# A two-layer hybrid trunk on one core: the key norm moved on VectorE, the chunk inverse packed to 32 columns

## The chip, the cores and the metric

One core of a Trainium2 chip runs the whole program. The metric is the device time of one execution in microseconds; with one core there is no slowest core to choose. Before the change it is 1543.94 us, the median of three runs (1543.90 to 1547.18).

## The reference, cut to what matters

The input x has 512 tokens of 1024 float32 numbers. Two layers run one after the other, each with a projection into two head groups, an output projection and a squared-ReLU MLP of width 4096, with residual adds. Layer 0 has an RWKV-7 group (8 heads of 64) and a gated DeltaNet group (8 heads of 64); layer 1 has sparse attention and block attention. The change touches layer 0 alone.

Both groups of layer 0 are recurrences over the tokens. The kernel computes them in chunks of 64 tokens. Of DeltaNet's form the reference says it plainly: with a lower triangular matrix of 64 x 64 per head and chunk,

```
a_mat = where(strict, (k_beta @ k.T) * decay, 0) + eye(64)
u = solve(a_mat, v * beta);  w = solve(a_mat, k_beta * exp(g))
v_new = u - w @ S;  o = (q * exp(g)) @ S + qk @ v_new
S = S * exp(g_last) + (k * exp(g_last - g)).T @ v_new
```

RWKV-7 in chunks has a matrix of the same shape (RWKV's own products instead of k_beta and k). Its key kk is divided by its length per head (`l2_normalize(k * k_k)`), and b = kk * a. The "bonus" adds sum(r * k * r_k) * v per head to its output.

## The kernel before, in words

Every engine has its own program, written out by hand, and semaphores tie them together; the order inside an engine's queue is fixed. Activations lie feature by feature: 128 features on the partitions, 512 tokens along them.

**The even projection.** 31 tiles of 128 columns go through PE (`tile`, L503, L504, L508: each weight is split by ACT into a high part, L1045, and by POOL into a low part, L1984; 24 matmuls of 512 columns). SP loads the weight of tile u once POOL has split tile u - 2 (L421). PE's order (L544 to L610) is: two LoRA tiles, ab, K, the LoRA products (L575), the gate products (L579), R, V, the chunk sums (L585 to L589, 32 moving columns), GQ (4 tiles), head sums for kk (`head_sums0`, L540), GK (4 tiles), head sums for gq, GV tile 0 (tile 23), the bonus sums (L540), the other GV tiles, head sums for gk, Z. There are 8 PSUM banks in turn; fill q waits until fill q - 8 has been read, so the last of the four bonus sums waits for ACT's first read of the gq sums (L1051), and the first three for DVE's convolutions of GK 1 to 3. DVE convolves each tile (`convolved`, L1453, L1469, L1471). ACT's queue is in the order of its loop over x (from L1076): at x = 20 to 23 the rounding of tile x + 3 (waits for PE's tile x), then the silu of GK tile x - 20 (L1064); at x = 23 also the squares of GK (L1059) and the inverse norm of gq (L1051 logarithm, L1054 exponential). At x = 19 it does the inverse norm of kk. DVE's three operations with that norm (kk scaled, L1545; b, L1546; a product of 128 x 32, L1548) stand behind the convolution of GK tile 0; the squares of kk, and then its norm, lie in the place of GV. Then come GK 1 to 3, GV 0, the bonus products (L1552) and the scaling of GQ (L1554).

**POOL's constants.** Between tile_lo(3) and tile_lo(6) POOL builds masks (L1967 to L2022): for each of six levels of the inverse a mask of 128 x 128 (a memset and selects), then MERGE, the six of them cut to each half's own 64 columns (L2018), and three small ones. Each waits for the one before.

**The even mixer** goes over blocks of 128 tokens (s = 0 to 3, with an extra turn for the tail). In each turn all engines interleave the matrices and inverse of block s ("ahead") with the state steps and outputs of block s - 1 ("behind"). A tile "by head" is 128 x 512: partition halves are the two chunks of the block, 8 heads of 64 columns. LTR and LTG hold the matrices of RWKV (R) and DeltaNet (G).

**The inverse** joins diagonal blocks: from blocks of 2 rows on to 64 in five levels (LEVELS = 6, the first is free). At the start DVE masks LTG and LTR to the first off-diagonals (L1630, L1641), POOL adds the identity (L2052), and DVE transposes Q into TI (L1652, `first_inverse`). Each level then does, for R and then G:

```
PE   below_blocks : bank[g] = LT.T-products with TI     (both_halves, L640, 16 matmuls 64x64 by 64x64)
ACT  below_blocks : XM = -bank[g]                       (L1189)
PE   joined_blocks: bank[g] = Q-products with XM        (L640)
DVE  joined_blocks: TI = where(mask, bank[g], TI)       (L1659), later Q = transpose(TI) (L1664)
```

The last level writes into Q itself, and `inv_done` then lets `turned_inputs` of the next block and `solved` go on. On DVE the joins of levels 1 to 4 stand between the outputs of block s - 1: `chunk_out` (L1698 to L1704), `decay_steps` (L1606), `out_var`, `out_scaled` (L1717, L1718), `scaled_rows` (L1611, L1612), `mixed` (from L1724). PE's state sums and chunk outputs of block s - 1 stand between levels 0 and 1. ACT's copy of the key values (L1175) stands ahead of `solved(m, 1)` and of the levels.

## Time and profile before

| | us |
|---|---|
| median of three runs | 1543.94 |
| the profiled execution | 1542.63 |
| its span | 1540.7 |
| busy: PE / DVE / ACT / POOL | 1440.3 / 677.3 / 605.4 / 571.3 |
| even projection, to PE's first matmul of the mixer | 0 to 220 |
| a projected tile: PE / DVE's convolution of it | 5.5 / 3.75 |
| mixer, starts of blocks s = 0, 1, 2, 3 | 220.0, 255.2, 305.1, 356.5 |
| mixer's end, output projection's first matmul | 443.3 |
| mean granted clock of TensorE over the span | 0.97 |

The profiled execution's time holds 1.9 us around its span. Engines overlap, so busy times don't add up to the span. A row of a timeline can merge several records ("x64"); a PE record's duration runs from its start to its modelled end, so the records of a batch overlap, and the step from one to the next is their total less the last one's duration, over one less than their number. Each matmul of 32-bit numbers leaves two records.

### The profile page before, as it was taken

To read this page: it belongs to the slowest core of one execution; us is meant where nothing else is said; L and a number is where in the kernel's file an instruction comes from. 1 tells how busy PE (TensorE), PEld (TensorE's weight loads), DVE (VectorE), ACT (ScalarE), POOL (GpSimd) and SP (SyncE) were. 2 spreads that over 40 slices of the span, in tenths; PEclk is the share of its full clock that TensorE was granted. 3 is DMA by queue.
4 is the path that set the end of the run, shared out by engine and by line. 5 is a ranking of instruction groups with operands and counts; after the bars stand their busy time and mean duration, and the time that the engine had idled before them with its cause. 6 is when DMAs were issued, how large, how long until landed. Compare 5 with 4: busy or idle time off the path is not lost.

```text
span 1540.7 us, 24474 instructions
## 1 busy us (share of the span) xinstructions
PE 1440.3 (93%) x10273; PEld 1153.7 (75%) x10273; DVE 677.3 (44%) x1059; ACT 605.4 (39%) x872; POOL 571.3 (37%) x265
## 2 busy tenths in 40 slices
PE   7999899888769999999999799978999999999998
PEld 5787568788758888888888687754468888888886
DVE  4675756777543413223143306868823314122231
ACT  5425453434354413223142435467834313232231
POOL 4543321101024343434334232417934343434341
PEclk9999899999779999999999899998999999999999
DMA  4332200000112323232323221210012323223231
GB/s 141 96 96 68 69 14 3 3 3 3 57 55 84 108 84 107 83 100 91 107 84 83 82 83 56 82 55 1 1 55 83 109 82 104 88 93 97 85 106 54
DMA packets 128392, 109.99 MB, mean 71 GB/s; under 512 B 10679, under 2 KB 126513, under 8 KB 128305
## 3 DMA queue, kind: packets, MB, share of 16 engines
q1 hardware_dynamic: 127712, 107.64, 22.6%
q8 instruction: 69, 1.13, 0.3%
q10 hardware_dynamic: 592, 1.07, 0.2%
q14 instruction: 19, 0.15, 0.0%
HBM read 106.60 MB, written 2.10 MB: 71 GB/s over the span
## 4 chain that ended last, share of the span: by engine, by line
PE 76%; DVE 11%; ACT 5%; POOL 3%; issue 3%; DMA 1%; DVEq 0%; ACTq 0%; SPq 0%; POOLq 0%
PE ps L503 21%; PE ps L508 21%; PE ps L504 21%; PE ps L640 5%; POOL lower L2093 2%; DVE lower L1880 2%; DVE lower L1876 1%; PE ps L655 1%; PE ps L648 1%; POOL pw_lo L1984 1%; DVE lower L1865 1%; ACT lower L1377 1%; PE ps L744 1%; PE ps L617 1%; PE ps L540 1%
## 5 line engine op out<-in xcount | busy, mean ns | idle before, releaser
L2061 POOL TENSOR_TENSOR w_lo<-lower,w_hi 128x2048 fp32r<-128x2048 f32 x84 | 387.8, 4616 | 634.7 <-ACT w_hi L1033 634.7
L503 PE MATMUL ps<-h_hi,w_hi 128*128 128x512 f32 x792 | 316.3, 399 | 8.9 <-ACT h_hi L1038 5.9
L504 PE MATMUL ps<-h_hi,w_lo 128*128 128x512 f32 x792 | 315.0, 398 | 0.0
L1033 ACT ACTIVATE w_hi<-lower 128x2048 fp32r<-128x2048 f32 x84 | 160.2, 1907 | 242.8 <-PE ps L508 242.8
L508 PE MATMUL ps<-h_lo,w_hi 128*128 128x512 f32 x792 | 201.6, 396 | 0.3
L503 PE MATMUL ps<-a_hi,w_hi 128*128 128x512 f32 x480 | 189.3, 394 | 0.0
L504 PE MATMUL ps<-a_hi,w_lo 128*128 128x512 f32 x480 | 189.2, 394 | 0.0
L503 PEld LDWEIGHTS ps<-h_hi,w_hi 128*128 128x128 f32 x792 | 150.5, 190 | 46.4 <-issue 11.5
L504 PEld LDWEIGHTS ps<-h_hi,w_lo 128*128 128x128 f32 x792 | 150.6, 190 | 36.0 <-issue 0.5
L508 PEld LDWEIGHTS ps<-h_lo,w_hi 128*128 128x128 f32 x792 | 148.9, 188 | 37.2 <-DVE h_lo L1582 1.7
L1825 DVE TENSOR_TENSOR lower<-lower,ps 128x512 f32<-128x512 f32 x64 | 44.0, 688 | 268.7 <-PE ps L508 268.7
L1809 DVE SCALAR_TENSOR_TENSOR lower<-ps,lower 128x512 f32<-128x512 f32 x64 | 44.3, 692 | 226.0 <-PE ps L508 209.9
L1264 ACT ACTIVATE lower<-lower 128x512 f32<-128x512 f32 x64 | 40.5, 633 | 215.9 <-DVE lower L1809 215.9
L508 PE MATMUL ps<-a_lo,w_hi 128*128 128x512 f32 x480 | 121.5, 395 | 0.0
L1984 POOL TENSOR_TENSOR pw_lo<-lower,pw_hi 128x1024 fp32r<-128x1024 f32 (+1 forms) x31 | 76.2, 2460 | 118.4 <-ACT pw_hi L1045 118.2
L508 PEld LDWEIGHTS ps<-a_lo,w_hi 128*128 128x128 f32 x480 | 90.3, 188 | 21.6
L504 PEld LDWEIGHTS ps<-a_hi,w_lo 128*128 128x128 f32 x480 | 90.2, 188 | 21.2
L503 PEld LDWEIGHTS ps<-a_hi,w_hi 128*128 128x128 f32 x480 | 90.1, 188 | 21.1
L1814 DVE TENSOR_TENSOR h_lo<-lower,h_hi 128x512 fp32r<-128x512 f32 x64 | 97.4, 1521 | 6.9 <-ACT h_hi L1266 6.9
L503 PE MATMUL ps<-x_hi,pw_hi 128*128 128x512 f32 (+1 forms) x232 | 94.4, 407 | 0.4 <-POOL pw_lo L1984 0.4
L504 PE MATMUL ps<-x_hi,pw_lo 128*128 128x512 f32 (+1 forms) x232 | 91.5, 394 | 0.0
L640 PE MATMUL ps<-lower 64*64 64x64 f32 x2112 | 73.4, 228 | 11.6 <-DVE lower L1659 7.9
(356 smaller groups left out, 1974.0 us busy)
## 6 DMA issues: line engine op xcount, KB each, us to landing
lower<-in_mlp_w_dram SPq DMA_DIRECT2D x64, 1024.0 KB, 5.4
lower<-in_ev_w_in_dram SPq DMA_DIRECT2D x30, 512.0 KB, 3.9
lower<-in_od_w_in_dram SPq DMA_DIRECT2D x10, 1024.0 KB, 5.1
lower<-in_ev_w_out_dram SPq DMA_DIRECT2D x4, 1024.0 KB, 5.1
lower<-in_od_w_out_dram SPq DMA_DIRECT2D x4, 1024.0 KB, 4.9
out_dram<-lower SPq DMA_DIRECT2D x4, 512.0 KB, 3.2
lower<-in_od_w_in_dram SPq DMA_DIRECT2D x6, 256.0 KB, 3.8
upper<-in_x_dram SPq DMA_DIRECT2D x1, 1024.0 KB, 7.2
```

The costliest lines, as they stand in the source:

```text
L503: pe.matmul(o, wh, xh, start=(i_ == 0), stop=False)
L504: pe.matmul(o, wl, xh, start=False, stop=False)
L508: mm = pe.matmul(o, wh, xl, start=False, stop=(i_ == n_ - 1))
L640: mm = pe.matmul(ps[part, b, h_ * HD:(h_ + 1) * HD], mats[part, j, q, :], vals[part, j, q, :], start=(start and h_ == 0), stop=True, skip_ ...
L1033: act.activation(WH[:, u % 2, :, 0:w], RAW[:, u % 2, :, 0:w], ACT.Copy).then_inc(hi_ready, 1)
L1264: act.activation(sq, sq, ACT.Square).then_inc(h1_sq, 1)
L1809: dve.scalar_tensor_tensor(out=SQT[:, b % 4, :], in0=src(q)[:, :], scalar=0.0, in1=RS[2 * l + 1], op0=ALU.max, op1=mul).then_inc(bank_read, 1)
L1814: dve.tensor_tensor(HL[:, b, :], SQT[:, b % 4, :], as_f32(HH[:, b, :]), sub).then_inc(h1_ready, 1)
L1825: dve.tensor_tensor(XT[:, k, :], XT[:, k, :], src(q_m2[l] + k)[:, :], add)\
L1880: t.step(dve.match_replace(sc, M8[:, i, :], sc, TAKEN))
L1984: pool.tensor_tensor(PWL[:, u % 3, :, 0:w], PRAW[:, u % 2, :, 0:w], as_f32(PWH[:, u % 3, :, 0:w]), ALU.subtract).then_inc(pw_lo, 1)
L2061: pool.tensor_tensor(WL[:, u % 2, :, 0:w], RAW[:, u % 2, :, 0:w], as_f32(WH[:, u % 2, :, 0:w]), ALU.subtract)\
```

## The change

Two things are changed. First, DVE's three operations with the norm of kk go from behind GK's tile 0 to behind the bonus products; the squares and the norm of kk get a place of their own (SQ_KKS), since GV is written before they are read. Second, of each 64 x 64 block matrix in the inverse only the 32 columns of its own diagonal block of 32 are kept (QC and TC, 128 x 256 for 8 heads), up to blocks of 32 rows. PE gets its stationary operand 64 columns wide with the other half zero (LD, and X in the place of QI), its moving operand is 32 wide (`in_halves`). ACT makes the wide form out of the packed one: two copies with a scale of 0 or 1 (or 0 or -1) per partition (`sides`). DVE's masked copies and transposes work on QC and TC. The masked copy now writes QC, and TC is its transpose. The last level joins the two blocks of 32 with 32 x 32 operands (`across`), after ACT has spread QC into QI (`inv_exp`), and DVE's last masked copy fills the lower left part. On the way in, ACT copies the left half and DVE overlays the right half by a masked copy (`diagonal`), ACT spreads both groups behind the key values (`spread`), and POOL's add of the identity waits for that. POOL builds five masks instead of six, JOIN, EYEQ and SIDE.

```diff
@@ -152,8 +152,11 @@
         INCL = flat(carve(P), P)
         o_merge = carve(LEVELS * P)
 
-        MERGE = grid(o_merge, LEVELS, HD)
-        INCLC, STRICTC, EYEC = (flat(o_merge + (LEVELS + i) * HD, HD) for i in range(3))
+        INCLC, STRICTC, EYEC = (flat(o_merge + i * HD, HD) for i in range(3))
+        HQ = HD // 2
+        JOIN = grid(o_merge + 3 * HD, LEVELS - 1, HQ)
+        EYEQ = flat(o_merge + 3 * HD + (LEVELS - 1) * HQ, HQ)
+        SIDE = flat(o_merge + 3 * HD + LEVELS * HQ, 4)
         SCANM = flat(carve(NC * CW), NC * CW)
         PC = flat(carve(P), P)
@@ -206,14 +209,14 @@
+        SQ_KKS = flat(carve(4 * PW), 4 * W)
-        SQ_KK, SQ_GQ = ([x[:, c, :] for c in range(4)] for x in (GV, Z))
+        SQ_KK, SQ_GQ = [SQ_KKS[:, c * W:(c + 1) * W] for c in range(4)], [Z[:, c, :] for c in range(4)]
         SQ_GK = [WA, GD, G2, LW2]
@@ -242,7 +245,8 @@
-        LTR, LTG, TIR, TIG, XMR, XMG, DT = (by_head(home("inverse")) for _ in range(7))
+        LTR, LTG, LDR, LDG, DT = (by_head(home("inverse")) for _ in range(5))
+        QCR, QCG, TCR, TCG = (home("inverse", 2 * P).rearrange("p (j q t) -> p j q t", j=PAIRS, q=2) for _ in range(4))
         MK = DT
+
+        def compact(x):
+            return x.rearrange("p j q t -> p (j q t)")[:, 0:2 * P].rearrange("p (j q t) -> p j q t", j=PAIRS, q=2)
+
+        def quarter(b):
+            return bank[b][:, 0:2 * P].rearrange("p (j q t) -> p j q t", j=PAIRS, q=2)
+
@@ -695,25 +706,44 @@
 
+            def in_halves(b, mats, vals):
+                for h_ in range(NH):
+                    j, q = h_ // 2, h_ % 2
+                    for part in HALVES:
+                        mm = pe.matmul(ps[part, b, h_ * HQ:(h_ + 1) * HQ], mats[part, j, q, :], vals[part, j, q, :],
+                                       start=True, stop=True)
+                return mm
+
...
+            def across(b, mats, vals, down):
+
+                for h_ in range(NH):
+                    j, q = h_ // 2, h_ % 2
+                    for k in range(2):
+                        first, second = (slice(k * HD + i * HQ, k * HD + (i + 1) * HQ) for i in range(2))
+                        rows, cols = (first, second) if down else (second, first)
+                        mm = pe.matmul(ps[cols, b, h_ * HQ:(h_ + 1) * HQ], mats[rows, j, q, :], vals[rows, j, q, :],
+                                       start=True, stop=True)
+                return mm
+
             def below_blocks(s, lev):
 
                 n = 2 * LAST * s + 2 * lev
-                for g, (lt, ti) in enumerate(((LTR, TIR), (LTG, TIG))):
+                for g, (lt, ld, tc) in enumerate(((LTR, LDR, TCR), (LTG, LDG, TCG))):
                     pe.wait_ge(inv_t, n + (2 if lev == 0 else g + 1))
-                    both_halves(g, lt, ti, True).then_inc(inv_x, 1)
+                    if lev < LAST - 1:
+                        pe.wait_ge(inv_ld, 2 * s + 2)
+                        in_halves(g, ld, tc).then_inc(inv_x, 1)
+                    else:
+                        across(g, lt[:, :, :, HQ:HD], tc, True).then_inc(inv_x, 1)
 
             def joined_blocks(s, lev):
                 n = 2 * LAST * s + 2 * lev
-                for g, (qi, xm) in enumerate(((QIR, XMR), (QIG, XMG))):
+                for g, (xe, ld, qc) in enumerate(((QIR[s % 2], LDR, QCR), (QIG[s % 2], LDG, QCG))):
                     pe.wait_ge(inv_xm, n + g + 1)
-                    if lev == 0:
-                        pe.wait_ge(inv_q0, 2 * s + 2)
+                    if lev < LAST - 1:
+                        in_halves(g, xe, qc).then_inc(inv_y, 1)
                     else:
-                        pe.wait_ge(inv_q, 2 * (LAST - 1) * s + 2 * (lev - 1) + g + 1)
-                    if lev < LAST - 1:
-                        both_halves(g, qi[s % 2], xm, True).then_inc(inv_y, 1)
-                    else:
-                        both_halves(g, xm, qi[s % 2], True).then_inc(inv_y, 1)
+                        across(g, compact(ld), qc, False).then_inc(inv_y, 1)
 
             def state_reads(s, k):
@@ -1183,10 +1213,30 @@
 
+            def sides(dst, src, neg, done):
+                act.activation(dst[:, :, :, 0:HQ], src, ACT.Copy, scale=SIDE[:, neg:neg + 1])
+                act.activation(dst[:, :, :, HQ:HD], src, ACT.Copy, scale=SIDE[:, neg + 1:neg + 2]).then_inc(done, 1)
+
+            def diagonal(s, g, lt, qc):
+                act.wait_ge(r_kk if g else r_lt, s + 1)
+                act.activation(qc, lt[:, :, :, 0:HQ], ACT.Copy).then_inc(inv_a, 1)
+
+            def spread(s):
+                for g, (ld, qc) in enumerate(((LDG, QCG), (LDR, QCR))):
+                    act.wait_ge(inv_c, 2 * s + g + 1)
+                    sides(ld, qc, 0, inv_ld)
+
             def below_blocks(s, lev):
-                for g, xm in enumerate((XMR, XMG)):
+                for g, (xe, ld) in enumerate(((QIR[s % 2], LDR), (QIG[s % 2], LDG))):
                     act.wait_ge(inv_x, 2 * LAST * s + 2 * lev + g + 1)
-                    act.activation(flat4(xm), bank[g], ACT.Copy, scale=-1.0).then_inc(inv_xm, 1)
+                    if lev < LAST - 1:
+                        sides(xe, quarter(g), 2, inv_xm)
+                    else:
+                        act.activation(compact(ld), quarter(g), ACT.Copy, scale=-1.0).then_inc(inv_xm, 1)
+                if lev == LAST - 1:
+                    for g, (qi, qc) in enumerate(((QIR[s % 2], QCR), (QIG[s % 2], QCG))):
+                        act.wait_ge(inv_q, 2 * (LAST - 1) * s + 2 * (LAST - 2) + g + 1)
+                        sides(qi, qc, 0, inv_exp)
 
             def out_squares(s):
@@ -1222,8 +1272,11 @@
                 if ahead:
+                    diagonal(s, 1, LTG, QCG)
                     lower_rows(s)
+                    diagonal(s, 0, LTR, QCR)
                     key_values(s)
+                    spread(s)
                 if behind:
                     solved(m, 1)
                 if ahead:
@@ -1540,16 +1593,15 @@
                 convolved("GK", c, 4 + c)
-                if c == 0:
-                    dve.wait_ge(rs_grp, 1)
-                    t.link(dve.tensor_tensor(wide(KK), wide(KK), wide(GV), mul))
-                    t.step(dve.tensor_tensor(wide(B), wide(KK), wide(B), mul))
-                    dve.wait_ge(l0_act, 1)
-                    dve.tensor_tensor(wide(EREST), wide(EREST), wide(BETA), mul)
             convolved("GV0", 0, 8)
             for c in range(4):
                 q = pq["bon"] + c
                 dve.tensor_tensor(BON[:, c, :], filled0(q), V[:, c, :], mul).then_inc(p_read[0], 1)
+            dve.wait_ge(rs_grp, 1)
+            t.link(dve.tensor_tensor(wide(KK), wide(KK), SQ_KKS, mul))
+            t.step(dve.tensor_tensor(wide(B), wide(KK), wide(B), mul))
+            dve.wait_ge(l0_act, 1)
+            dve.tensor_tensor(wide(EREST), wide(EREST), wide(BETA), mul)
             dve.wait_ge(rs_grp, 2)
             dve.scalar_tensor_tensor(out=wide(GQ), in0=wide(GQ), scalar=float(HD) ** -0.5,
                                      in1=wide(Z), op0=mul, op1=mul)
@@ -1627,7 +1679,6 @@
                 dve.tensor_tensor(GRK[s], product_of(0, 0), GRK[s], mul).then_inc(r_kk, 1)
-                dve.tensor_tensor(QIG[s % 2], LTG, mask(MERGE[:, 0, :]), mul).then_inc(inv_m, 1)
@@ -1638,30 +1689,42 @@
-                dve.tensor_tensor(QIR[s % 2], LTR, mask(MERGE[:, 0, :]), mul).then_inc(inv_m, 1)
...
+            def of_quarter(x):
+                return x.unsqueeze(1).unsqueeze(1).broadcast_to([P, PAIRS, 2, HQ])
+
+            def on_side(i):
+                return SIDE[:, i:i + 1].bitcast(I32).unsqueeze(1).unsqueeze(1).broadcast_to([P, PAIRS, 2, HQ])
...
+            def diagonal(s, g, lt, qc, tc):
+                dve.wait_ge(inv_a, 2 * s + g + 1)
+                dve.copy_predicated(qc, on_side(1), lt[:, :, :, HQ:HD]).then_inc(inv_c, 1)
+                dve.wait_ge(inv_c, 2 * s + g + 1)
+                dve.tensor_tensor(tc, qc, of_quarter(JOIN[:, 0, :]), mul).then_inc(inv_m, 1)
+
             def first_inverse(s):
-                for g, (ti, qi) in enumerate(((TIG, QIG), (TIR, QIR))):
+                for g, (tc, qc) in enumerate(((TCG, QCG), (TCR, QCR))):
                     dve.wait_ge(inv_q0, 2 * s + g + 1)
-                    dve.transpose(flat4(ti), flat4(qi[s % 2])).then_inc(inv_t, 1)
+                    dve.transpose(flat4(tc), flat4(qc)).then_inc(inv_t, 1)
 
             def joined_blocks(s, lev):
                 n = 2 * LAST * s + 2 * lev
                 inner = lev < LAST - 1
-                for g, x in enumerate((TIR, TIG) if inner else (QIR[s % 2], QIG[s % 2])):
+                for g, (qc, qi) in enumerate(((QCR, QIR[s % 2]), (QCG, QIG[s % 2]))):
                     dve.wait_ge(inv_y, n + g + 1)
-                    dve.copy_predicated(x, blocks(MERGE[:, lev + 1, :]), by_head(bank[g]))\
-                       .then_inc(inv_t if inner else inv_done, 1)
+                    if inner:
+                        dve.copy_predicated(qc, of_quarter(JOIN[:, lev + 1, :].bitcast(I32)), quarter(g))\
+                           .then_inc(inv_q, 1)
+                    else:
+                        dve.wait_ge(inv_exp, 2 * s + g + 1)
+                        dve.copy_predicated(qi[:, :, :, HQ:HD], on_side(0), quarter(g)).then_inc(inv_done, 1)
                 if inner:
-                    for g, (ti, qi) in enumerate(((TIR, QIR), (TIG, QIG))):
-                        dve.wait_ge(inv_t, n + 2 + g + 1)
-                        dve.transpose(flat4(qi[s % 2]), flat4(ti)).then_inc(inv_q, 1)
+                    for g, (tc, qc) in enumerate(((TCR, QCR), (TCG, QCG))):
+                        dve.wait_ge(inv_q, 2 * (LAST - 1) * s + 2 * lev + g + 1)
+                        dve.transpose(flat4(tc), flat4(qc)).then_inc(inv_t, 1)
@@ -1741,10 +1804,12 @@
                     lower_products(s)
+                    diagonal(s, 0, LTG, QCG, TCG)
                 if behind:
                     state_sums(m, 0)
                 if ahead:
                     key_products(s)
+                    diagonal(s, 1, LTR, QCR, TCR)
                 if behind:
                     state_reads(m, 1)
                 if ahead:
@@ -1996,16 +2061,15 @@
-            for lev in range(1, LEVELS):
+            for lev in range(1, LEVELS - 1):
                 if lev == 3:
                     tile_lo(4)
                 b = 1 << lev
-                last = int(lev == LEVELS - 1)
-                low = FULL[:, lev, :].rearrange("p (n q w) -> p n q w", q=2, w=b)[:, :, last, :]
-                t.link(pool.memset(low, 1.0))
-
-                select(low, 0 if last else -b, [[-2 * b, P // (2 * b)], [0, b]], 1, 0.0)
-                select(low, b - 1 if last else 2 * b - 1, [[2 * b, P // (2 * b)], [0, b]], -1, 0.0)
+                right = FULL[:, lev, :].rearrange("p (n q w) -> p n q w", q=2, w=b)[:, :, 1, :]
+                t.link(pool.memset(right, 1.0))
+
+                select(right, 0, [[-2 * b, P // (2 * b)], [0, b]], 1, 0.0)
+                select(right, b - 1, [[2 * b, P // (2 * b)], [0, b]], -1, 0.0)
             tile_lo(5)
             for g in range(16):
@@ -2015,10 +2079,15 @@
             for part in HALVES:
-                t.link(pool.tensor_copy(MERGE[part], FULL[part, :, part]))
                 t.link(pool.tensor_copy(INCLC[part], INCL[part, part]))
                 t.link(pool.tensor_copy(EYEC[part], IDENT[part, part]))
             t.link(pool.tensor_tensor(STRICTC, INCLC, EYEC, ALU.subtract))
+            for i in range(4):
+                rows = slice(i * HQ, (i + 1) * HQ)
+                t.link(pool.tensor_copy(JOIN[rows], FULL[rows, 0:LEVELS - 1, rows]))
+                t.link(pool.tensor_copy(EYEQ[rows], IDENT[rows, rows]))
+                for at_, v_ in enumerate((1 - i % 2, i % 2, i % 2 - 1, -(i % 2))):
+                    t.link(pool.memset(SIDE[rows, at_:at_ + 1], float(v_)))
@@ -2047,9 +2116,11 @@
                     pool.memset(SG, 0.0).then_inc(e_state, 1)
-                for g, qi in enumerate((QIG, QIR)):
+                for g, (qc, tc) in enumerate(((QCG, TCG), (QCR, TCR))):
                     pool.wait_ge(inv_m, 2 * s + g + 1)
-                    pool.tensor_tensor(qi[s % 2], qi[s % 2], of_heads(EYEC), ALU.add).then_inc(inv_q0, 1)
+                    pool.wait_ge(inv_ld, 2 * s + g + 1)
+                    pool.tensor_tensor(qc, tc, EYEQ.unsqueeze(1).unsqueeze(1).broadcast_to([P, PAIRS, 2, HQ]),
+                                       ALU.add).then_inc(inv_q0, 1)
```

## Rows read from the trace of the kernel before

**Rows 1.** The page: the chain that ended last, share of the span.

```profile
PE 76%; DVE 11%; ACT 5%; POOL 3%; issue 3%; DMA 1%; DVEq 0%; ACTq 0%; SPq 0%; POOLq 0%
```

**Rows 2.** Timeline 149 to 176: start us, us, engine, line, operation [idle before].

```profile
149.72 2.29 DVE L1545 TENSOR_TENSOR lower<-lower,upper 128x2048 f32<-128x2048 f32 x1 [6.95 <-ACT upper L1054]
...
156.34 2.33 DVE L1548 TENSOR_TENSOR lower<-lower 128x32 f32<-128x32 f32 x1
...
162.99 1.04 ACT L1045 ACTIVATE pw_hi<-lower 128x1024 fp32r<-128x1024 f32 x1
...
164.27 1.02 PE L540 MATMUL ps<-upper,lower 128*128 128x512 f32 x2
...
169.94 0.63 ACT L1064 ACTIVATE upper<-upper 128x512 f32<-128x512 f32 x1 [2.17 <-DVE upper L1471]
...
174.10 2.06 ACT L1051 ACTIVATE upper<-ps 128x512 f32<-128x512 f32 x4
...
174.75 2.07 PE L540 MATMUL ps<-upper,lower 128*128 128x512 f32 x2 [2.71 <-ACT upper L1051]
```

**Rows 3.** Timeline 38 to 60, POOL's constants and the gate matmuls.

```profile
39.00 0.15 POOL L2005 MEMSET lower<- 128x64 f32 x1
...
42.84 0.12 POOL L2015 MEMSET lower<- 128x24 f32 x1
43.02 0.50 POOL L2018 COPY lower<-lower 64x384 f32<-64x384 f32 x1
...
58.93 1.52 PE L579 MATMUL ps<-upper 128*128 128x512 f32 x3 [0.16 <-ACT upper L1105]
```

**Rows 4.** Windows: busy us (records) by engine, PEclk; one in s = 0.

```profile
233.00:234.00 1.00, 0.97 (x18) 0.98 (x20) 0.00 (x0) 0.00 (x0) 0.23 (x1) 0.50 0.00 0
```

**Rows 5.** Timeline 230 to 243, the first inverse levels (s = 0).

```profile
230.95 1.27 POOL L2052 TENSOR_TENSOR upper<-upper,lower 128x512 f32<-128x512 f32 x1 [1.25 <-DVE upper L1641]
...
232.40 0.60 ACT L1175 ACTIVATE lower<-ps 128x512 f32<-128x512 f32 x1 [4.54 <-PE ps L640]
...
233.03 3.68 PE L640 MATMUL ps<-lower 64*64 64x64 f32 x64 [0.66 <-DVE lower L1652]
...
238.81 2.09 PE L640 MATMUL ps<-lower 64*64 64x64 f32 x64
...
239.59 1.29 DVE L1664 STREAM_TRANSPOSE upper<-lower 128x512 f32<-128x512 f32 x2
240.00 0.60 ACT L1189 ACTIVATE lower<-ps 128x512 f32<-128x512 f32 x1 [2.65 <-PE ps L640]
...
241.88 0.73 DVE L1659 COPY_PREDICATED lower<-lower,ps 128x512 f32<-128x512 int32 x1 [1.00 <-PE ps L640]
242.66 0.95 PEld L640 LDWEIGHTS ps<-lower 64*64 64x64 f32 x30
```

**Rows 6.** Timeline of PE near 107, the chunk sums with 32 moving columns.

```profile
107.13 0.43 PE L589 MATMUL ps<-lower 128*64 128x32 f32 x8
```

**Rows 7.** Groups by form, PE: line, operation, shapes, count | busy us, mean ns.

```profile
L640 PE MATMUL ps<-lower,upper 64*64 64x64 f32 x704 | 24.7, 221 | 0.0
...
L589 PE MATMUL ps<-lower 128*64 128x32 f32 x8 | 0.4, 228 | 0.0
```

**Rows 8.** Groups by form, ACT and DVE: 512 and 256 elements.

```profile
L1318 ACT ACTIVATE lower<-ps 128x256 f32<-128x256 f32 x8 | 3.1, 383 | 13.3 <-PE ps L508 13.3
L1211 ACT ACTIVATE upper<-ps,lower 128x512 f32<-128x512 f32 x4 | 2.8, 709 | 0.0
...
L1677 DVE TENSOR_TENSOR upper<-upper,lower 128x256 f32<-128x256 f32 x7 | 3.0, 422 | 5.2 <-PE ps L655 5.2
...
L1625 DVE TENSOR_TENSOR upper<-lower 128x512 f32<-128x512 f32 x4 | 2.8, 692 | 0.1
```

**Rows 9.** Timeline of DVE in s = 1: output sums, last masked copies.

```profile
288.59 0.65 DVE L1698 TENSOR_TENSOR lower<-lower 128x512 f32<-128x512 f32 x1
...
303.61 1.39 DVE L1659 COPY_PREDICATED lower<-lower,ps 128x512 f32<-128x512 int32 x2
```

More of the change, by code:

```diff
@@ L206, in trunk_kernel @@
         SQ = [None] + [grid(o_ring + 4 * W, KT, W)] * 3
-        carve(4 * PW)
+        SQ_KKS = flat(carve(4 * PW), 4 * W)
         o_pl = carve(KT * W)
@@ L359, in trunk_kernel @@
              "e_sqg e_sqr e_var e_ln e_rstd e_on r_tr r_tg").split())
-        (inv_m, inv_q0, inv_x, inv_xm, inv_y, inv_t, inv_q, inv_done) = (sem(n) for n in (
-            "inv_m inv_q0 inv_x inv_xm inv_y inv_t inv_q inv_done").split())
+        (inv_a, inv_c, inv_ld, inv_m, inv_q0, inv_x, inv_xm, inv_y, inv_t, inv_q, inv_exp, inv_done) = (
+            sem(n) for n in "inv_a inv_c inv_ld inv_m inv_q0 inv_x inv_xm inv_y inv_t inv_q inv_exp inv_done".split())
         LAST = LEVELS - 1
@@ L1640, in key_products @@
                 dve.tensor_tensor(RK[s], product_of(0, 1), mask(INCLC), mul).then_inc(r_kd, 1)
-                dve.tensor_tensor(QIR[s % 2], LTR, mask(MERGE[:, 0, :]), mul).then_inc(inv_m, 1)
-            def blocks(m):
-                return m.bitcast(I32).unsqueeze(1).unsqueeze(1).broadcast_to([P, PAIRS, 2, HD])
+            def of_quarter(x):
+                return x.unsqueeze(1).unsqueeze(1).broadcast_to([P, PAIRS, 2, HQ])
+            def on_side(i):
+                return SIDE[:, i:i + 1].bitcast(I32).unsqueeze(1).unsqueeze(1).broadcast_to([P, PAIRS, 2, HQ])
             def flat4(x):
                 return x.rearrange("p j q t -> p (j q t)")
+            def diagonal(s, g, lt, qc, tc):
[3 more added lines that the diff above has]
+                dve.tensor_tensor(tc, qc, of_quarter(JOIN[:, 0, :]), mul).then_inc(inv_m, 1)
             def first_inverse(s):
-                for g, (ti, qi) in enumerate(((TIG, QIG), (TIR, QIR))):
+                for g, (tc, qc) in enumerate(((TCG, QCG), (TCR, QCR))):
                     dve.wait_ge(inv_q0, 2 * s + g + 1)
-                    dve.transpose(flat4(ti), flat4(qi[s % 2])).then_inc(inv_t, 1)
+                    dve.transpose(flat4(tc), flat4(qc)).then_inc(inv_t, 1)
             def joined_blocks(s, lev):
```

## The prediction, made before the changed kernel ran

> **What bounds the kernel now.** I read the page first: PE holds 76% of the chain that ended last [rows 1], so a change counts only where PE is made to wait or its own work moves. Then I read the timeline around the three places that the diff touches: the tail of the even projection, the constants that POOL builds early on, and the inverse levels of the even mixer. Last came the prices, from the groups by form. The profiled execution took 1542.63 us (span 1540.7); the median of the runs shown is 1543.94, so it stands 1.3 us below. My sum is made against 1542.63. A measurement of this kernel can tell about 0.2%, 3.1 us, from no change.
>
> **Part A, the key norm behind the bonus sums.** Before, DVE idles 6.95 us for ACT's norm, and is then held by three operations from 149.72 to 158.67, one of them a 128x32 product of 2.33 us beside POOL's own work [rows 2]. The projections of GK 1 to 3 queue behind that, and ACT's silus and squares behind them: ACT starts its last GK silu at 169.94 and the norm of GQ at 174.10, and only that read frees the bank for the last bonus sum, which PE gives at 174.75, after 2.71 us idle [rows 2]. PE had its first bonus sum out at 164.27. After the change DVE convolves each GK tile as PE ends it, since its work for a tile (3.75 us) is shorter than PE's (5.5). What ends last then is ACT's queue: its weight rounding ahead of that silu waits for PE to finish tile 23, just ahead of 164.3. From there ACT needs 1.05 (a rounding, 1.04 at 162.99), then, as before, 4.8 us from that silu to the bank's release (169.94 to 174.75). So the last bonus sum starts at 164.3 + 1.05 + 4.8 = 170.15: **4.6 us earlier**. The moved operations now stand between the bonus products and the scaling of GQ: 2.3 + 2.3 + 0.2 us from about 172, with no POOL work beside them, done at 176.8; PE needs 5.5 us from 171.3 for the next projected tile, so what hides them is that tile, and they cost nothing. If that cover goes (8.9 us as before), DVE is up to 4 us late for one tile, whose bank PE wants only eight fills later, and gains 1.7 back on each of the next two. Bounds for the part: 3 to 6.
>
> **Part B1, the constants.** POOL gives up the last level's build (39.00 to 39.85, 0.85) and two copies of 0.57 each, 1.99 in all, and adds per quarter of the partitions a copy of 160 elements, one of 32 and four memsets, each waited for. A waited-for memset costs 0.18 (42.84 to 43.02); the 64x384 copy took 0.50 [rows 3], from which I take 0.38 and 0.27 for the copies with their waits: 4 x (0.38 + 0.27 + 0.72) = 5.5. POOL's next roundings thus come 3.5 us later. On them hang a weight load on SP's queue, ACT's rounding and the sigmoids behind it, and these are what the gate matmuls at 58.93 wait for, with just 0.16 us idle ahead [rows 3]. PE has no slack to give back until 164: **+3.5**. Bounds 1 (memsets as in an unwaited row) to 4.
>
> **Part B2, the batches of a level.** Each product of a level is a batch of 16 matmuls in 32 records, half of the moving columns gone (64 to 32), the stationary operand still 64 columns wide. Now 64 records take 2.09 us (at 238.81), of which the last is 0.22: 0.030 each, some 0.93 a batch [rows 5, 7]. The nearest row for 32 moving columns under 64 stationary ones is the small sums at 107.13: 8 records in 0.43, the last 0.23, again 0.029 each [rows 6, 7]. So I take 0.93 for a batch after the change; the other end is half, 0.47. The price at 32 columns looks set by the weight load. The Trainium skill (TensorE: Matmul & The Clock Gate, "Wait — 56ns, not 53.3ns?") has a floor of about 25 ns from start to start; as an estimate by that page a batch would be 0.80, and each interval below 0.4 shorter, some 2 us less in all.
>
> **The chain of a level.** Now it is 238.81 to 242.66, 3.85 us [rows 5]: batch for R to ACT 1.19 (240.00), copy 0.60, batch to DVE 1.21, masked copy 0.73, and PE starts at once, since TI is what DVE has just written; the transposes run beside PE. After the change DVE writes Q, and the next level's first product needs its transpose, which stands on DVE behind the masked copies of both groups. ACT's one copy becomes two of 256 elements with a scale from memory: a plain one is 0.38, the scale adds 0.11 (0.709 against 0.60), they overlap by 0.1: 0.90 a pair [rows 5, 8]. DVE's operations fall by 0.27 each (512 elements 0.69, 256 elements 0.42): masked copy 0.46, transpose 0.43 [rows 5, 8]. From the first transpose's end: PE 0.06, first batch 0.93; second batch to ACT 1.19, so ACT at 2.18; pair to 3.08; PE from 3.14; to DVE 1.21, 4.35; masked copy 0.46 overlapping the transpose by 0.1, then 0.43: **5.14 against 3.85**, +1.29 for each interval that nothing covers. With half batches (0.47) it would be 4.1.
>
> **First tile block (s = 0), nothing beside it.** Entry: DVE's second half per group (masked copy, wait, product: 0.95) replaces a product of 0.6, behind an added ACT copy of 0.4; together some 1.1 until the key values' copy, now at 232.40, then at 233.5. Behind it ACT spreads both groups (2 x 0.9, done 235.9), POOL may add the identity to R only then (1.27 now [rows 5], 0.7 at half the size), then a transpose 0.43: the first level starts at about 237.1 instead of 233.03: +4.0. Level 0 ran at the granted clock 0.50 [rows 4] and took 5.78 (233.03 to 238.81); with half the columns its batches should be load-bound at either clock, 5.14: -0.6. Three intervals at +1.29: +3.9. Last level: 32-wide stationary operands and one plain 256 copy, but the final masked copy waits for four spreading copies: about -0.8. Sum **+6.5**.
>
> **Later blocks.** Here other work covers the levels. In s = 1 DVE is busy without a gap from 288.59 to the final masked copies at 303.61 [rows 9]. Up to level 0 the block gains 0.9 us of added DVE and ACT work, level 0 another 0.5, level 1's longer interval 1.3, less 2.0 saved in DVE's shorter operations: DVE starts its output sums at about 289.3, +0.7, and as these and the products after them stay in one queue, those masked copies, and with them the block, come +0.6. For s = 2 I take the same less 1.4 for a stretch at the lower clock that the shorter gap ahead of level 3 should avoid; for s = 3, without the next block's work on DVE, -0.6. Sum of the three: -0.8, and B2 is **+5.7**, bounds -8 (half batches) and +13 (every interval uncovered, 12 more at 1.29 less what the columns save).
>
> **Sum.** -4.6 + 3.5 + 5.7 = +4.6, so 1547.2 against the profiled execution, 1548.5 against the median; I give 1548.
>
> **Rivals.**
> *Half batches, faster.* If streaming columns, not the weight load, set the batch, it is 0.47 in each of 16 intervals. For: the rows of the levels, all with 64 columns on both sides, fit either cause. Against: the 32-column row. The point is about 0.75 us a batch: below it PE and ACT fall out of the chain, DVE starts its output sums some 3 us sooner in each later block, and its own saving (20 operations at 0.27 a block) counts. B2 is then +3.0 at s = 0 and about -11 in the other three, -8; total -4.6 + 3.5 - 8 = -9.1: 1534. Chance 0.2.
> *The constants are hidden.* Tile 6's rounding has 1.4 us of slack at PE, and if the memsets cost 0.04 each as in an unwaited row, POOL's delay is 1 us: total +1 to +2, 1544. Chance 0.12.
> *The clock falls in the levels.* PE's idle share in a level goes from none to about a quarter; if the granted clock is 0.50 through most of it, the transposes and state products at up to twice the time add 2 to 3 us a block: 1557. For: the clock did fall at 231, after lighter work [rows 4]. Against: it came back during level 0. Chance 0.08.
> *The forecast:* 0.6, its own range 1543 to 1553.
>
> **Numbers.** Faster by over 0.2% (under 1540.9): 0.05 of the forecast, nearly all of the half batches, a little of the third: 0.23. Within: 0.3 of the forecast, most of the hidden constants: 0.26. Slower: 0.51. The range 1536 to 1556 reaches from the middle of half batches to the falling clock.
>
> **What would show it.** Part A: the key products on DVE after the bonus products, no DVE wait near 142, the last bonus sum some 4.6 us after tile 23's end plus 1.3. B1: the gate matmuls with an idle of 3 us ahead, POOL's memsets at 0.18. B2: 64x32 records at 0.029 apart, an interval of 5.1 in s = 0 with the transpose as its last link, first level about 4 us later; blocks s = 1 to 3 within 1.5 us of their old length. I am wrong if a batch takes 0.5 to 0.6, if an interval in s = 0 is under 4.3, or if blocks s = 1 to 3 shrink by 3 us each.

## The result: 3.6% slower, and the profile after

The changed kernel takes 1600.67 us (median of four runs, 1597.08 to 1602.88) against 1543.92 (1542.04 to 1547.18): ratio 1.0363 with an interval of 1.0341 to 1.0385. I had forecast 1548, and no more than 1556. The profiled run took 1598.54 us, 55.9 more than the profiled one of before.

The page, sections 2 (tenths in 40 slices of 40 us) and 4, and the group of the packed products:

```profile
PE   7999978889886999999999799996989999999998
PEclk9999985765857999999999899997999999999999
PE 79%; DVE 9%; ACT 5%; POOL 3%; issue 2%; DMA 1%; DVEq 0%; ACTq 0%; SPq 0%; POOLq 0%
L713 PE MATMUL ps<-lower 64*64 64x32 f32 x1536 | 74.9, 268 | 11.6 <-DVE lower L1727 7.9
```

PE's share of the chain went up, from 76% [rows 1] to 79%. The second line points at the reason: in most slices of the mixer the granted clock is five to eight tenths. Windows over the mixer show it closer (each row: the window, its length, PE busy us and records, PEclk, DMA share, GB/s):

```profile
218.00:230.00 12.00, 7.28 (x128) 0.94 0.00 1
230.00:235.00 5.00, 1.50 (x29) 0.50 0.00 0
250.96:258.88 7.92, 7.04 (x128) 0.50 0.01 2
266.80:271.40 4.60, 3.46 (x128) 0.50 0.02 4
280.00:290.00 10.00, 7.45 (x229) 1.00 0.01 2
295.00:305.00 10.00, 10.00 (x192) 0.50 0.01 3
308.10:313.20 5.10, 4.23 (x137) 1.00 0.01 3
313.90:337.80 23.90, 21.52 (x384) 0.50 0.01 2
```

The clock falls at about 229, close to where it fell before [rows 4], but then stays at 0.50 (1.2 of 2.4 GHz) for 48 us, and it falls again in every later block. An interval is the time from the first product of a level to that of the next. One interval of the first block and the start of the next, timeline of all engines:

```profile
258.05 0.44 DVE L1719 COPY_PREDICATED lower<-lower,ps 128x256 f32<-128x256 int32 x1 [1.26 <-PE ps L713]
258.39 0.76 DVE L1727 STREAM_TRANSPOSE lower<-lower 128x256 f32<-128x256 f32 x2
258.88 3.63 PE L713 MATMUL ps<-lower 64*64 64x32 f32 x64 [0.88 <-DVE lower L1727]
260.85 0.47 ACT L1217 ACTIVATE upper<-ps,lower 128x256 f32<-128x256 f32 x1 [5.38 <-PE ps L713]
261.22 0.47 ACT L1218 ACTIVATE upper<-ps,lower 128x256 f32<-128x256 f32 x1
...
262.32 3.60 PE L713 MATMUL ps<-lower,upper 64*64 64x32 f32 x64
...
266.80 1.43 PE L724 MATMUL ps<-lower 32*32 32x32 f32 x45 [0.88 <-DVE lower L1727]
```

64 records take 3.63 us, some 0.054 each, a batch of 32 records 1.72; the interval is 7.92 us where it was 3.85 [rows 5]. The transpose is its last link, as forecast; ACT's pair took 0.84 (forecast 0.90), masked copy 0.44, transposes 0.43 as far as PE waits. Only the batches are off. The group's shortest records, where the clock was at 1.00, took 0.19 instead of 0.29.

The two early parts (POOL's last copies and memsets, then PE's first matmul behind them; then the last bonus sum):

```profile
48.13 0.31 POOL L2087 COPY lower<-lower 32x160 f32<-32x160 f32 x1
48.51 0.21 POOL L2088 COPY lower<-lower 32x32 f32<-32x32 f32 x1
48.78 0.55 POOL L2090 MEMSET lower<- 32x1 f32 x4
...
52.08 0.47 PE L514 MATMUL ps<-x_hi,pw_hi 128*128 128x512 f32 x1 [1.78 <-POOL pw_lo L2049]
173.24 1.37 PE L551 MATMUL ps<-upper,lower 128*128 128x512 f32 x2 [3.28 <-ACT upper L1081]
```

Matched by their place in PE's order, the products of after stand 0.7 us later than before by 32 us (before the first row of rows 3, where the two kernels part), 2.7 in the tile that starts at 52.08, 2.9 from the gate products at 61.87 to the first bonus sum at 167.22, 1.5 **earlier** at the last bonus sum (173.24), 2.0 earlier from 173.8 to the mixer, and 55.9 later at the output projection. So the constants cost 2.0, and another 0.2 comes at the gate products, as it does in a_alone, which leaves the constants alone. The key norm gave 5.0, 4.5 of it at the last bonus sum, and the mixer lost 58.

Where each block lost, with the experiments beside it (start of the mixer, us; lengths of the blocks; the last one runs to the output projection's first matmul; each row is the profiled execution, which can stand some us off the median):

| kernel | start | s = 0 | s = 1 | s = 2 | s = 3, tail | mixer |
|---|---|---|---|---|---|---|
| before | 220.0 | 35.2 | 49.9 | 51.4 | 86.8 | 223.3 |
| after | 218.0 | 53.4 | 63.3 | 65.2 | 99.3 | 281.3 |
| packed_wide | 218.6 | 42.8 | 53.6 | 55.8 | 94.7 | 247.0 |
| packed_wide2 | 216.8 | 43.4 | 54.4 | 54.1 | 91.3 | 243.3 |
| short_columns | 219.5 | 47.0 | 54.5 | 54.5 | 94.3 | 250.3 |
| long_chain | 222.3 | 42.4 | 53.5 | 51.5 | 90.2 | 237.5 |
| after_fill | 216.7 | 59.8 | 56.3 | 51.8 | 92.0 | 260.0 |
| packed_filled | 217.6 | 42.8 | 51.1 | 51.1 | 88.8 | 233.8 |
| a_alone | 213.4 | 34.8 | 49.9 | 51.2 | 89.5 | 225.4 |
| a_fill | 213.8 | 33.6 | 51.3 | 51.2 | 89.7 | 225.8 |
| fill_only | 221.0 | 33.3 | 51.4 | 52.6 | 80.8 | 218.1 |
| a_fill2 | 216.2 | 33.3 | 49.9 | 51.4 | 82.3 | 216.8 |

### The profile page after: what moved, and what is told of

It reads as the page before. It is cut to its first block, busy times and chain, and to the rows that moved or that the text cites. A ratio compares the mean times of both kernels' runs of the same rounds, so it can differ in the third digit from the quotient of the medians.

```text
span 1596.8 us, 24581 instructions
## 1 busy us (share of the span) xinstructions
PE 1491.4 (93%) x10273; PEld 1202.0 (75%) x10273; DVE 655.3 (41%) x1067; ACT 626.9 (39%) x944; POOL 567.0 (36%) x284
## 4 chain that ended last, share of the span: by engine, by line
PE 79%; DVE 9%; ACT 5%; POOL 3%; issue 2%; DMA 1%; DVEq 0%; ACTq 0%; SPq 0%; POOLq 0%
PE ps L514 21%; PE ps L519 21%; PE ps L515 21%; PE ps L713 6%; POOL lower L2164 2%; DVE lower L1945 2%; PE ps L666 1%; PE ps L651 1%; DVE lower L1941 1%; PE ps L628 1%; PE ps L659 1%; ACT lower L1430 1%; PE ps L724 1%; POOL pw_lo L2049 1%; PE ps L551 1%
## 5 line engine op out<-in xcount | busy, mean ns | idle before, releaser
L514 PEld LDWEIGHTS ps<-h_hi,w_hi 128*128 128x128 f32 x792 | 150.4, 190 | 46.5 <-issue 11.5
L2049 POOL TENSOR_TENSOR pw_lo<-lower,pw_hi 128x1024 fp32r<-128x1024 f32 (+1 forms) x31 | 73.0, 2357 | 116.5 <-ACT pw_hi L1075 116.3
L519 PEld LDWEIGHTS ps<-a_lo,w_hi 128*128 128x128 f32 x480 | 90.2, 188 | 21.7
L514 PE MATMUL ps<-x_hi,pw_hi 128*128 128x512 f32 (+1 forms) x232 | 94.3, 407 | 2.2 <-POOL pw_lo L2049 2.2
L713 PE MATMUL ps<-lower 64*64 64x32 f32 x1536 | 74.9, 268 | 11.6 <-DVE lower L1727 7.9
```

What stands on the lines that cost most here:

```text
L514: pe.matmul(o, wh, xh, start=(i_ == 0), stop=False)
L519: mm = pe.matmul(o, wh, xl, start=False, stop=(i_ == n_ - 1))
L713: mm = pe.matmul(ps[part, b, h_ * HQ:(h_ + 1) * HQ], mats[part, j, q, :], vals[part, j, q, :], start=True, stop=True)
L2049: pool.tensor_tensor(PWL[:, u % 3, :, 0:w], PRAW[:, u % 2, :, 0:w], as_f32(PWH[:, u % 3, :, 0:w]), ALU.subtract).then_inc(pw_lo, 1)
```

## The experiments

Four kernels first, to part the columns from the chain and the key norm from both.

**packed_wide**: the packed products of levels 0 to 3 move 64 columns again; the second 32 are a copy that nobody reads. The edit of PE's product (cut: ACT and DVE skip the second 32 when they read the bank):

```diff
-                        mm = pe.matmul(ps[part, b, h_ * HQ:(h_ + 1) * HQ], mats[part, j, q, :], vals[part, j, q, :],
+                        mm = pe.matmul(ps[part, b, h_ * HD:(h_ + 1) * HD].rearrange("p (a t) -> p a t", a=2),
+                                       mats[part, j, q, :],
+                                       vals[part, j, q, :].unsqueeze(1).broadcast_to([HD, 2, HQ]),
...
```

> The changed kernel, with the moving operand of levels 0 to 3 read twice, so that each product moves 64 columns again (the second 32 of each 64 in PSUM are read by nobody). Same instructions, same chain. Theory A (32 moving columns are what keeps the granted clock at 0.50): the clock is 1.00 again in most of the levels, an interval in the first block is 5.1 to 5.4 us instead of 7.9, the mixer ends some 50 us earlier, 1545 to 1552. Theory B (the longer chain, in which PE idles a quarter of the time, is what lets the clock fall): the clock and the intervals stay, 1590 to 1603. Theory C (both count): in between.

1564.09 us, ratio 1.0129 (1.0113 to 1.0145). A little over a third of the loss is left, so the time lies between theories A and B, where theory C had it, and the columns alone are worth 36.6 us. The first block shows how. Timeline, then windows:

```profile
242.41 2.08 PE L716 MATMUL ps<-lower 64*64 64x64 f32 x64 [0.88 <-DVE lower L1732]
247.45 2.08 PE L716 MATMUL ps<-lower 64*64 64x64 f32 x64 [0.88 <-DVE lower L1732]
...
257.55 2.38 PE L729 MATMUL ps<-lower 32*32 32x32 f32 x128 [0.88 <-DVE lower L1732]
261.45 1.19 PE L680 MATMUL ps<-upper,lower 128*128 128x512 f32 x1 [1.53 <-DVE upper L1728]
```

```profile
245.00:250.00 5.00, 4.12 (x133) 1.00 0.01 3
312.00:317.00 5.00, 4.37 (x70) 0.50 0.00 0
330.00:335.00 5.00, 3.32 (x68) 0.68 0.01 3
```

Twice the columns, and the interval is 5.04 us instead of 7.92, at the full clock. My forecast was 5.14. But behind the last level of a block (312) and ahead of level 0 (330) the clock still falls. Half of each stationary operand is zero here as in the changed kernel, so those zeros are not what keeps the clock down.

**short_columns**: the kernel before, with 32 of 64 columns moved in levels 0 to 3. It leaves out the right half of each product, so its inverse is not the reference's; the chain and the order are those of before.

```diff
-                    both_halves(g, lt, ti, True).then_inc(inv_x, 1)
+                    (left_only(g, lt, ti) if lev < LAST - 1 else both_halves(g, lt, ti, True)).then_inc(inv_x, 1)
```

> The kernel before, where levels 0 to 3 compute only the left 32 of each head's 64 columns (the right ones keep what the bank held, so the inverse isn't the reference's); the chain, the copies and the order are those of before. Theory A: the clock falls to 0.50 in the levels as in the changed kernel, where a batch takes 1.72 instead of 0.93 us; an interval in the first block goes from 3.85 to about 7, total 1575 to 1595. Theory B: PE idles no more than before, so the clock and the time stay, 1541 to 1546.

1569.28 us (two runs), ratio 1.0163 (1.0143 to 1.0184), 6 us under the range that I gave for theory A. Timeline and windows:

```profile
246.16 3.60 PE L702 MATMUL ps<-lower 64*64 64x32 f32 x64
249.57 3.60 PE L702 MATMUL ps<-lower,upper 64*64 64x32 f32 x64
252.99 3.60 PE L702 MATMUL ps<-lower 64*64 64x32 f32 x64
```

```profile
230.00:262.00 32.00, 31.38 (x586) 0.50 0.01 3
290.00:295.00 5.00, 5.00 (x180) 1.00 0.01 3
305.00:315.00 10.00, 8.89 (x166) 0.50 0.01 2
```

PE is busy for 31.38 of 32 us and stays at 0.50 all the while; the kernel before, with 64 columns, had the full clock back in its first level: 3.68 us for the first 64 records, 2.09 from 238.81 on [rows 5]. So it isn't PE's waiting that keeps the clock down here. And at 0.50 a 32-column record takes 0.0534 (3.415 us for 64), as a 64-column one does. In later blocks, entered at the full clock, the same products keep it through levels 0 to 2 but for 3.4 us around the start of level 0 (290 to 295 is one window of it). In level 3, behind a wait of 2.9 us, it is at 0.50 in each of them (305 to 315); before, behind the same wait, it fell for 3.4 us at most.

**long_chain**: 64 columns, but PE waits for the transpose too.

```diff
                     pe.wait_ge(inv_t, n + (2 if lev == 0 else g + 1))
+                    if lev > 0:
+                        pe.wait_ge(inv_q, 2 * (LAST - 1) * s + 2 * (lev - 1) + g + 1)
```

> The kernel before, where PE's first product of levels 1 to 4 waits for the transpose of its group too, as the changed kernel makes it do; all operands keep 64 columns. An interval becomes 3.85 + 0.73 + 0.70 = 5.3 us, close to the changed kernel's 5.1 at the full clock. Theory A: the clock keeps what it was before, and the price is that of the chain, 3 x 1.4 to 4 x 1.4 us in the first block and little in the others, 1548 to 1553. Theory B: the clock falls to 0.50 in the levels, intervals of 7 to 8 us, 1580 to 1600.

1557.44 us (two runs), ratio 1.0087 (1.0065 to 1.0109). Timeline and window of the first block:

```profile
243.45 2.08 PE L640 MATMUL ps<-lower 64*64 64x64 f32 x64 [1.51 <-DVE upper L1666]
248.90 2.08 PE L640 MATMUL ps<-lower 64*64 64x64 f32 x64 [1.50 <-DVE upper L1666]
240.00:264.00 24.00, 17.73 (x574) 0.99 0.01 3
```

PE is busy 17.7 of 24 us, less than in the changed kernel, and keeps the full clock. Theory B falls: the longer chain by itself doesn't bring the clock down in levels 1 to 3, but for one stretch of 3.4 us at 305. The interval is 5.45 and the time 4 us above what I gave; 2.3 of it came before the mixer, in a stretch that the edit doesn't touch.

**a_alone**: the first part of the change on the kernel before (the diff ahead of the prediction, its hunks with SQ_KKS and DVE's moved lines).

> The kernel before with the first part of the change alone: DVE's three operations with the key norm behind the bonus products, squares in SQ_KKS. The order of PE's products in the changed kernel shows 4.7 us gained between the gate products and Z. My theory: nothing later gives it back, since it lies ahead of the levels, so 4.6 us under the kernel before, 1539.3 beside 1543.9 (ratio 0.997). Rival: an earlier entry into the mixer only lengthens a wait there (loads of the output weights, POOL's rows), then within 1.5 us of before.

1540.62 us (eleven runs), ratio 0.9980 (0.9971 to 0.9990): some 3 us, 4.5 at most, where I gave 4.6. Its last bonus sum comes at 170.29, my 170.15. Windows of before, then of a_alone:

```profile
170.00:180.00 10.00, 7.29 (x14) 0.54 0.20 53
410.00:425.00 15.00, 12.41 (x195) 0.55 0.26 85
425.00:440.00 15.00, 4.65 (x107) 0.73 0.21 70
```

```profile
170.00:180.00 10.00, 9.71 (x41) 1.00 0.13 38
405.00:425.00 20.00, 14.89 (x251) 0.59 0.08 26
425.00:440.00 15.00, 3.17 (x11) 0.50 0.22 71
```

The clock is at 1.00 at 170 to 178, where before had 0.50, so the mixer begins 6.6 us earlier; the last block then takes 2.7 us longer, its outputs at 0.50 where before had a stretch at 1.00 from 425 on. The output projection starts 4.5 us earlier, and the profiled execution took 1538.07, 4.6 under that of before. Why the medians lie only 2.6 apart no trace shows.

Three more to see whether the clock is the whole of it. **packed_wide2** doubles the columns of the last level too (the same edit in `across`, the last level's products).

> As packed_wide (1564.1), with the last level's 32 x 32 products reading their moving operand twice too, so that they move 64 columns. In packed_wide the granted clock was 0.50 behind the last level of each block (260 to 265, 315 to 317), and the blocks behind the first came out 3 to 5 us longer each than before. Theory A (few columns in the last level): the clock stays at 1.00 into the next block, 1 to 3 us less per block, 1555 to 1560. Theory B (PE's wait for the spreading copies and the final masked copies): the clock falls there as before the edit, 1562 to 1566.

1561.22 us, ratio 1.0128 (1.0108 to 1.0147): not to be told from packed_wide. Windows:

```profile
255.00:265.00 10.00, 8.32 (x194) 1.00 0.01 2
275.00:285.00 10.00, 8.12 (x144) 0.67 0.01 2
330.00:340.00 10.00, 8.13 (x156) 0.69 0.01 3
```

The clock does hold into the next block (255 to 265), as theory A had it, but it is lost at 275, ahead of level 0, where PE waits 2.3 us for DVE's key products, which stand behind the added `diagonal`. The wider last level costs time of its own: its first 128 records took 2.38 us in packed_wide and 3.58 here, both at 1.00. So the time is inconclusive, the clock is not.

**after_fill**: the changed kernel with fillings, products that nobody reads, in PE's waits.

```diff
+            def filler(b, at, n):
+                for i in range(n):
+                    pe.matmul(ps[:, b, at + i * P:at + (i + 1) * P], IDENT, INCL, start=True, stop=True)
...
                         across(g, lt[:, :, :, HQ:HD], tc, True).then_inc(inv_x, 1)
+                filler(3, 0, 1)
...
                         across(g, compact(ld), qc, False).then_inc(inv_y, 1)
+                filler(3, 0, 2)
+                filler(3, 2 * P, 1)
```

> The changed kernel with products that nobody reads, in a bank that is free there: one of 128 moving columns behind the second product of each half level, two more of them at its end, in PE's waits for ACT and DVE; the kernel's own instructions are untouched. If the clock is what costs the time, it comes back to 1.00 in the levels and the time goes from 1600.7 to 1550 to 1570, though PE has more to do. If the packed form costs the time by its chain, the extra products only add: 1605 or more.

1581.07 us (1575.94 to 1588.07), ratio 1.0259 (1.0236 to 1.0282): more work for PE, and 19.6 us less, though 11 above the range that I gave for a clock at 1.00 in the levels. Windows of the profiled execution (1575.94, the shortest of the four):

```profile
240.00:270.00 30.00, 30.00 (x430) 0.50 0.01 2
300.00:400.00 100.00, 91.20 (x2378) 0.99 0.01 3
```

From 240 to 270 PE is never idle and the clock does not come back; in the first block the fillings cost 6.4 us. From 302 to 404 it holds, and the blocks s = 1 to 3 fall from 227.8 to 200.2 us in sum. So with the kernel's own products untouched the clock's return gives back time, more than the fillings cost.

**packed_filled**: packed_wide2 with fillings ahead of and behind the key values, behind the state reads, and in the levels.

> packed_wide2 (1561.2) with products that nobody reads in PE's waits: ahead of and behind the key values, behind the state reads, and one and three in each level. It is to hold the granted clock at 1.00 through all four blocks, so that what is left against the kernel before is the price of the packed form's longer chain alone. By my sum for that (B2 +5.7, constants +2.0 and key norm -4.7 as the traces showed) it would be 1546 to 1550. Rival: the blocks behind the first lose some 3 us each by DVE's and ACT's added operations ahead of level 0 at any clock, 1553 to 1558.

1549.69 us (1548.64 to 1550.64), ratio 1.0037 (1.0022 to 1.0052). Windows:

```profile
217.00:260.00 43.00, 38.04 (x859) 1.00 0.01 2
260.00:311.00 51.00, 49.47 (x1234) 1.00 0.01 3
311.00:362.00 51.00, 49.47 (x1233) 1.00 0.01 3
417.00:451.00 34.00, 16.38 (x296) 0.67 0.20 66
```

With the clock at 1.00 until 422 the packed form, fillings included, costs 10.5 us in the mixer (the table), and the kernel lands 1.7 us from my forecast. That is in part luck: the mixer's term came out 4.8 dearer than I gave, the constants 1.5 cheaper, and the fillings stretch an interval of the first block from 5.04 to 5.39 us. Also, the kernel before isn't at the full clock throughout. Against a_fill2 below, whose first block is, the first block costs 9.5 us (42.8 for 33.3), the next two 1.2 and -0.3.

The same cure for the kernel before. **a_fill** (four products ahead of and four behind the first key values, 30 behind the last outputs, 10 behind the last turns, on a_alone), then **a_fill2** with more places:

```diff
+                        if lev == 3 and behind:
+                            filler(3, 9)
...
                 if not ahead:
-                    filler(0, 30)
+                    filler(0, 44)
```

and 10, 4, 2 and 3 products in the last block's waits between state reads, `solved` and state sums.

> a_alone with the same kind of products that nobody reads at three places where the kernel before loses the clock: four ahead of and four behind the key values of each first block (PE waits there for DVE and ACT), 30 behind the last block's outputs and 10 behind its last turns (PE waits 10.35 and 2.95 us there). If the clock holds: level 0 of the first block takes 3.9 instead of 5.4 us (1.5 us), the output projection starts at 1.00 (2.5 us, its products 0.23 instead of 0.43 apart for 5 us), so 4 us under a_alone's 1540.6: 1536 to 1537. Rival: the filling delays the key values or the turns by as much as it gives, 1539 to 1542.

> a_fill (1537.8) with more of them: nine ahead of level 3 in the later blocks (PE waits 2.8 us there), ten, four, two and three in the waits of the last block's state steps, 44 instead of 30 behind its outputs. If each holds the clock: 1 us for each of two blocks, 4 us in the state steps (0.053 apart at 0.50 against 0.030), 1.5 us at the output projection's start: 1530 to 1533. Rival: the fillings end later than the waits they fill, since one takes 0.23 us at the full and 0.45 at the half clock: 1537 to 1540.

a_fill: 1537.76 us, ratio 0.9967 (0.9951 to 0.9983), just above the 1536 to 1537 that I gave. The first level starts at 226.77 and takes 3.86 us, but the 30 products were done 4.5 us before PE's turn came, and the clock was at 0.50 again. a_fill2: 1531.94 us, ratio 0.9924 (0.9911 to 0.9937); again, beside fill_only:

> a_fill2 once more, beside fill_only on the same chip: 1530 to 1533 if its first result holds.

> The kernel before with a_fill2's unread products, without the moved key norm: what the clock alone gives. a_fill2 stood 12.4 us under before, a_alone 2.6. If the two add, 9.8 us under before, 1534. If the key norm's gain was partly given back in a_alone by the half clock in the last block's state steps (its blocks began 7 us earlier than before, its output projection only 4.5), the parts give more together than apart, and this one comes out at 1536 to 1539.

1532.09 us (0.9916, 0.9898 to 0.9934), and fill_only 1535.45 (0.9941, 0.9924 to 0.9957). Windows of a_fill2:

```profile
216.00:249.00 33.00, 29.67 (x808) 1.00 0.01 3
400.00:433.00 33.00, 31.04 (x476) 1.00 0.30 97
433.00:440.00 7.00, 7.00 (x29) 1.00 0.01 2
```

But for two stretches of 3.4 us (at 318 and 369) the clock is at 1.00 from the first block into the output projection, which starts at 432.97 instead of 443.32 with its products at full pace at once. Against the 1543.21 of before, measured beside them, the fillings alone give 7.8 us, a_alone gave 2.6, and both give 11.1: nearly their sum. That they give more together (the second case of that expectation) isn't shown. In the traces the fillings save 6.0 us in the last block, 1.9 in the first and 2.2 in the output projection's first 14 us, and cost 2.7 in s = 1 and 2 (the table, fill_only). **a_fill2 beats both kernels**, 11 to 12 us (0.8%) under before and 69 under after. What it adds is PE work that nobody reads.

## Why the prediction was wrong

- **Part A: right.** The last bonus sum came 4.5 us earlier where I gave 4.6; 0.5 more at the products behind it came with the clock. The moved operations cost PE nothing, as forecast: the 2.0 us are still there at the mixer's start (218.0 for 220.0). Alone the part is worth 2.6 us in the medians; in its trace the last block gives 2.7 back to the clock, and I had not looked past the mixer's entry.
- **B1: too dear.** +2.0 for 3.5. The added build took 4.9 us (44.45 to 49.38) of the 5.5 that I summed, so POOL's next rounding began 3.1 us later (49.58 for 45.79, less the 0.7), and 1.1 of that was slack at tile 6's products, where PE now idles 1.78 us. The rival that hid the constants is wrong too; its sum was also off, since +1 to +2 on the median is 1545 to 1546, not 1544.
- **Entry of the first block: right.** From the mixer's start (2.0 us earlier) the key values' copy came 1.2 us later than before (231.54 for 232.40) and the first level 4.1 later (235.12 for 233.03): I gave 1.1 and 4.0.
- **The chain of an interval: right at the full clock.** 5.04 in packed_wide for 5.14, and the mixer of packed_filled, with the clock held and the cost of its fillings in it, is +10.5, 2.0 of it in a last block whose tail is at half clock, where I gave B2 +5.7 with an upper bound of 13; by block +7.6, +1.2, -0.3, +2.0 for my +6.5, +0.6, -0.8, -0.6.
- **The step that failed** is "with half the columns its batches should be load-bound at either clock, 5.14". At the full clock the batch is load-bound, as I had it: half batches, the other rival, are out (0.030 a record in the levels of short_columns at 1.00, as with 64 columns). But the load is not one price: 64 weight columns take 0.030 us a record at 1.00 and 0.0534 at 0.50, and `across`, with 32 of them, 0.027 at 0.50 (3.46 us for 128 records). The Trainium skill (TensorE: Matmul & The Clock Gate, "LDWEIGHTS (loading the stationary operand)") gives a load as its columns over 1.2 GHz, 53 ns for 64: the trace agrees at 0.50 and shows about half at 1.00. So level 0 took 7.92, not 5.14, and so did the three intervals behind it.
- **The rival that came true had a chance of 0.08 and a fifth of its price.** I held against it that the clock came back in level 0 of the kernel before, with 64 columns moved per product; I carried that over to 32. short_columns shows that it does not come back with 32 in the first block, even with PE busy 31.4 of 32 us. I priced the fall at 2 to 3 us a block for transposes and state products; the levels themselves were the larger part, four intervals at 7.92 for 5.04, 11.5 us in a block that is at half clock throughout. The rival stood 9 us over the forecast. The mixer lost 58 us, by an estimate some 47 of them to the clock (58.0 less the 10.5 of packed_filled, which has fillings and 64 columns).
- In the later blocks columns and chain seem to work together. With 64 columns and the long chain (packed_wide, long_chain) levels 1 to 3 there ran at 1.00 but for the one stretch in long_chain. With 32 and the short chain (short_columns) levels 1 and 2 did, and level 3 ran at 0.50. With both (after, s = 1) the clock fell at 293.5, just ahead of level 0, came back at 307 in the state products, so that level 1 ran at 1.00 (308 to 313), and was at 0.50 again through levels 2 and 3 (314 to 338), with no wait of PE above 0.9 us ahead of that fall. What exactly lets the clock fall is left open; the runs only show what changed it.

## What to carry to other kernels

Packing an operand to fewer moving columns saved TensorE nothing here, where the weight load set the pace, and it took the full clock away; ask of every stretch at which clock its rows were taken, and whether the edited work would still bring it back. Price each TensorE term at both levels, and let the fall be a rival in which every TensorE row of the stage, the edited batches above all, has its price at the low clock. Where PE waits beside a chain that it must resume quickly, products that nobody reads, sized to end inside the wait, can be worth more than a shorter wait: here 7.8 us against 2.6. They have to fill the wait to its end: in a_fill a gap of 4.5 us behind them was followed by the half clock.

## What the runs showed that I had not expected

A busy PE does not by itself get the full clock back: 31.4 of 32 us busy at 0.50 in short_columns, 30.0 of 30 in after_fill, while the full clock was kept with 17.7 of 24 us busy in long_chain. And shortening one wait came with another clock elsewhere: in a_alone 170 to 178 is free of the half clock and the stretch at 1.00 behind 425 is lost.
